# A two-layer hybrid trunk on one core: more seven-product chunks in the Down stages, a split wait at the block heads, and dilated copies ahead of a split

## What is computed

```python
def conv_ffn(h, w_up, conv_w, conv_b, w_down):
    u = h @ w_up                       # 2048 -> 11264
    ...                                # causal depthwise convolution of width 3
    gate, val = jnp.split(u, 2, axis=-1)
    return (jax.nn.silu(gate) * val) @ w_down   # 5632 -> 2048
```

## Time and profile before

| what | value |
|---|---|
| median of 3 runs | 2505.23 us (2504.09 to 2505.72) |
| the profiled execution, device time | 2504.78 us |
| its span in the profile | 2503.0 us |
| TensorE matmuls | 2495.3 us busy, 11847 |
| VectorE | 2106.8 us busy, 84% |
| ScalarE | 1422.0 us busy, 57% |
| granted TensorE clock | 1.00, the 2.4 GHz level, in every slice |

### The profile page before, as it was taken

The page is one execution under the profiler, slowest core; times in us unless marked ns, Lnnn a source line. Parts: engine busy times, 40 slices in busy tenths (PEclk is TensorE's granted clock), DMA queues, the critical chain, the costliest instruction groups (busy, mean ns, idle before and its releaser), DMA issues.

```text
span 2503.0 us, 30597 instructions
## 1 busy us (share of the span) xinstructions
PE 2495.3 (100%) x11847; PEld 2093.8 (84%) x11847; DVE 2106.8 (84%) x2373; ACT 1422.0 (57%) x1535; POOL 28.9 (1%) x36
## 2 busy tenths in 40 slices
PE   9999999999999999999999999999999999999999
PEld 8988988888888888888888888888888888888887
DVE  6656666999999999998778888776699999999998
ACT  6545555655656566556545545544566665666654
POOL 1000000000000000000000000000000000000000
PEclk9999999999999999999999999999999999999999
DMA  8554554646455557576556666654465655645654
GB/s 282 185 159 159 185 194 137 233 152 235 168 195 193 190 187 245 169 227 192 157 162 188 187 202 182 187 168 152 141 231 172 221 183 170 217 168 202 238 173 161
DMA packets 362227, 472.28 MB, mean 189 GB/s; under 512 B 18997, under 2 KB 215813, under 8 KB 361968
## 3 DMA queue, kind: packets, MB, share of 16 engines
q1 hardware_dynamic: 360448, 465.64, 56.9%
q0 software_dynamic: 1408, 4.76, 0.6%
q10 hardware_dynamic: 240, 0.10, 0.0%
HBM read 468.31 MB, written 3.68 MB: 189 GB/s over the span
## 4 chain that ended last, share of the span: by engine, by line
PE 93%; DVE 3%; ACT 2%; issue 1%; DMA 1%; SPq 0%
PE psum L1907 41%; PE psum L1911 20%; PE psum L1793 8%; PE psum L1794 8%; PE psum L1800 8%; PE psum L2005 1%; DVE w_lo L1078 1%; PE psum L1918 1%; PE psum L1920 1%; PE psum L1919 1%; PE psum L2130 1%; DMA w_raw<-in_f_w_up 1%; PE psum L2094 0%; PE psum L2128 0%; PE psum L1749 0%
## 5 line engine op out<-in xcount | busy, mean ns | idle before, releaser
L1907 PE MATMUL psum<-w_hi,xT 128*128 128x512 f32 x4016 | 1000.4, 390 | 0.3 <-DVE phase L1141 0.3
L1907 PEld LDWEIGHTS psum<-w_hi,xT 128*128 128x128 f32 x4016 | 751.5, 188 | 155.6 <-DVE phase L1141 0.7
L632 ACT ACTIVATE w_hi<-w_raw 128x2048 fp32r<-128x2048 f32 (+1 forms) x342 | 618.7, 1816 | 365.2 <-PE psum L1911 267.6
L1078 DVE TENSOR_TENSOR w_lo<-w_raw,w_hi 128x2048 fp32r<-128x2048 f32 (+1 forms) x342 | 732.1, 2162 | 57.6 <-ACT w_hi L632 57.2
L1911 PE MATMUL psum<-w_lo,xT 128*128 128x512 f32 x2008 | 523.8, 389 | 0.1
L1911 PEld LDWEIGHTS psum<-w_lo,xT 128*128 128x128 f32 x2008 | 376.8, 188 | 79.1 <-DVE w_lo L1078 1.0
L1793 PE MATMUL psum<-w_hi,xT 128*128 128x512 f32 (+1 forms) x1008 | 362.0, 369 | 0.0
L1794 PE MATMUL psum<-w_hi,xT 128*128 128x512 f32 (+1 forms) x1008 | 355.9, 363 | 0.0
L1086 DVE TENSOR_TENSOR w_lo<-w_raw,w_hi 128x2048 fp32r<-128x2048 f32 (+1 forms) x118 | 255.9, 2180 | 54.8 <-ACT w_hi L643 54.5
L643 ACT ACTIVATE w_hi<-w_raw 128x2048 fp32r<-128x2048 f32 (+1 forms) x118 | 215.3, 1830 | 104.1 <-PE psum L1911 58.8
L1070 DVE TENSOR_TENSOR w_lo<-w_raw,w_hi 128x2048 fp32r<-128x2048 f32 (+1 forms) x98 | 188.7, 1941 | 59.5 <-ACT w_hi L621 59.0
(11 more groups left out here) (199 smaller groups left out, 1887.5 us busy)
## 6 DMA issues: line engine op xcount, KB each, us to landing
w_raw<-in_f_w_up SPq DMA_DIRECT2D x352, 512.0 KB, 4.9
w_raw<-in_f_w_down SPq DMA_DIRECT2D x176, 512.0 KB, 5.1
w_raw<-in_b_w_qkv SPq DMA_DIRECT2D x192, 256.0 KB, 4.0
w_raw<-in_a_w_qkv SPq DMA_DIRECT2D x94, 512.0 KB, 4.5
w_raw<-in_b_w_qkv SPq DMA_DIRECT2D x256, 128.0 KB, 2.6
w_raw<-in_a_w_o SPq DMA_DIRECT2D x16, 1024.0 KB, 5.0
w_raw<-in_b_w_qkv SPq DMA_DIRECT2D x32, 512.0 KB, 6.3
w_raw<-in_b_w_o SPq DMA_DIRECT2D x16, 1024.0 KB, 5.0
```

The source lines that it names most:

```text
L632: nc.scalar.activation(w_hi[:, slot, cols], w_raw[:, slot, cols], ACT.Copy).then_inc(hi_ready, 1)
L1078: nc.vector.tensor_tensor(w_lo[:, slot, cols], w_raw[:, slot, cols], w_hi[:, slot, cols], ALU.subtract).then_inc(lo_ready, 1)
L1907: pe.matmul(o, x[:, h, P * m:P * (m + 1)], hi, start=start and h == 0, stop=False)
```

## The change

Three edits.

First, the form of the Down passes: groups of two where there were groups of three, so pass 0 has seven and pass 1 eight seven-product chunks. They now stand at pairs 6, 8, 10, 12, 14, 16, 18 and at 3, 6, 8, 10, 12, 14, 16, 18. The stage has 59 entries instead of 57.

Second, the first operation of `combine` increments a semaphore of its own, `p6_out`. TensorE waits for that at the head of an Up block and of Down, and for `combined` only before the second half of the head's first plain chunk (`upper_free`), eight matmuls later.

Third, in VectorE's `b_head` the copy `b_take` stands ahead of the split of entry 6.

```diff
-DOWN_ENTRIES = [(what, p, j) for p, form in enumerate(((6, (2, 2, 3, 3, 2, 3)), (3, (3, 2, 2, 3, 3, 2, 3)))) for what, j in down_pass(*form)]
+DOWN_ENTRIES = [(what, p, j) for p, form in enumerate(((6, (2, 2, 2, 2, 2, 2, 3)), (3, (3, 2, 2, 2, 2, 2, 2, 3)))) for what, j in down_pass(*form)]
...
-                chain.step(nc.vector.tensor_tensor(u[:, 1, :], p6, u[:, 0, :], ALU.add))
-                chain.settle()
+                nc.vector.tensor_tensor(u[:, 1, :], p6, u[:, 0, :], ALU.add).then_inc(p6_out, 1)
+                dve.wait_ge(p6_out, tg + 1)
...
                 for e in range(B_HEAD):
                     if e == 0 and is_turn(h, 0):
                         split_b(c + LEAD)
+                    if e == 3:
+                        b_take(c + e, h, odd)
                     if e + LEAD + 1 == B_ONES[0]:
                         b_add_weights(c + B_ONES[0], c + B_SUMS[0])
                     split_ahead(c, e)
...
-                    if e == 3:
-                        b_take(c + e, h, odd)
...
-            def plain_square(c, x, own, start, stop, high_made, low_made):
+            def plain_square(c, x, own, start, stop, high_made, low_made, upper_free=None):
                 high_made()
                 for half, i, tile in SQUARE:
+                    if half == 1 and i == 0 and upper_free is not None:
+                        upper_free()
...
+                def upper_free():
+                    at_least(pe, combined, tg)
...
             def up_block(layer, n, c, t):
                 tg, odd = UP_BLOCKS * layer + t, t % 2
-                if t > 0:
-                    pe.wait_ge(combined, tg)
+                at_least(pe, p6_out, tg)
...
                     if e == 0:
-                        pe.wait_ge(combined, last)
+                        pe.wait_ge(p6_out, last)
...
                     elif what == "std":
-                        plain_square(c + e, x, own, j == 0, False, high_made, low_made)
+                        def upper_free():
+                            pe.wait_ge(combined, last)
+
+                        plain_square(c + e, x, own, j == 0, False, high_made, low_made, upper_free if e == 0 else None)
```

More of the change, by code:

```diff
@@ L357, in trunk @@
         mix_ready, mix_hi, mix_lo = sem("mix_ready"), sem("mix_hi"), sem("mix_lo")
-        p1_out, combined, u_summed = sem("p1_out"), sem("combined"), sem("u_summed")
+        p1_out, p6_out, combined, u_summed = sem("p1_out"), sem("p6_out"), sem("combined"), sem("u_summed")
         dve_chain = sem("dve_chain")
@@ L1978, in fast_sum, with up_entry_of @@
                 low(x[1], 1, c, 3, psum[:, own + 1, :]).then_inc(used, 1)
-            def up_entry_of(c, t, e, own, other):
+            def up_entry_of(c, t, tg, e, own, other):
                 def high_made():
@@ L1988, in up_entry_of @@
                 what, j = UP_ENTRIES[t][e]
+                def upper_free():
+                    at_least(pe, combined, tg)
                 x = [xT[:, 2 * j + i, :, :] for i in range(2)]
                 if what == "std":
-                    plain_square(c, x, own, j == 0, 2 * j + 2 == KB, high_made, low_made)
+                    plain_square(c, x, own, j == 0, 2 * j + 2 == KB, high_made, low_made, upper_free if j == 0 else None)
                 else:
@@ L2023, in up_block @@
                         pe.wait_ge(val_taps, tg)
-                    up_entry_of(c + e, t, e, up_bank(layer, odd), up_bank(layer, 1 - odd))
+                    up_entry_of(c + e, t, tg, e, up_bank(layer, odd), up_bank(layer, 1 - odd))
                     if t == 0:
```

## The result

The changed kernel takes 2515.79 us in the median of 6 runs (2513.3 to 2518.24), the kernel before 2505.25 in runs beside it: ratio **1.0043**, 95% interval 1.003 to 1.0056. It is slower, by 10.5 us. A second set of runs on another occasion gave 2515.17 against 2505.59, ratio 1.0039 (1.0025 to 1.0052).

The account below looks back on a forecast made before the run. TensorE, busy over the whole span, bounds the kernel, until VectorE's lead in Down runs out. 2504.8 - 2.7 - 0.3 - 1.1 + 12.1 = 2512.8, on the median's scale 2513.2, stated as 2513.0 us; range 2508.0 to 2517.0.

Parts of the forecast that it names:

- 12 matmuls, -2.7 us: Down stages: one more seven-product chunk per pass, two passes, two layers, takes 12 matmuls of 0.2265 us off TensorE.
- VectorE's run of 11.45 us: Down, group of two: VectorE needs 11.45 us without an idle, TensorE 10.20, so each run eats 1.25 us of lead.
- The waits, 11.5 us: TensorE waits before chunks 14, 16, 18 of Down: 2.96 us in pass 0, 2.79 in pass 1, two layers.
- hand-over and restart: Extra loss in the Down passes around TensorE's waits, estimated at 0.15 us per pass, 0.6 us in all.
- Nothing is carried on: After chunk 18 VectorE idles some 4.1 us against 3.3 to 3.5 lacking, so pass 1 and the dilated heads begin as before.
- Head's wait 0.3: Head of an Up block and of Down: waiting for the first extras operation only removes the L1141 wait, gain 0.3 us.
- dilated copies 1.1: Dilated head 0: the bank copy ahead of the 2.29 us split removes TensorE's 1.07 us wait, gain 1.1 us.
- cost 0: Dilated heads 1 to 7: softmax starts 0.9 us later but has 3.9 us of cover; at most 6 us without it.
- Rival 1: Chunks 12 to 18 of each Down pass: VectorE's run fits within its lead, nothing stalls, 2501.1 us; chance 0.08.
- rival 4: VectorE's Down run costs full instruction durations, 12.0 us, losing 5.3 us a pass, about 2522 us; chance 0.02.
- Rival 2: Down "one" entries: TensorE's tight wait is the low weights, not the mixed copy; about 2504.7 us, no change; chance 0.06.
- Rival 3: Late loads stall VectorE's 24 sums after runs of two, 0.3 us each, 7 us more, 2520 us; chance 0.09.

Follow-up runs that it names:

- pass0_only: The changed kernel with the old Down form in pass 1, so the new form in pass 0 alone: 2509.41 us against 2505.59 for the kernel before, ratio 1.0015.
- copy_first: The changed kernel with VectorE's mixed copy L1470 ahead of the split of the same "one" entry: 2514.19 us against 2505.85 for the kernel before, ratio 1.0033.

## Why the prediction was right

Forecast 2513.0 (2508.0 to 2517.0), slower; measured 2515.79. Term by term:

- **12 matmuls, -2.7 us.** 11835 of them, as counted.
- **VectorE's run of 11.45 us.** It is 11.45 after, in every dense stretch, and the leads of 2.04 and 2.21 us at chunk 10 run out where they were said to, before chunk 14. Twelve waits, three per pass.
- **The waits, 11.5 us.** 11.4 by the distances of starts. The hand-over and restart was set at 0.15 per pass and came out larger. It comes with each of the twelve waits and not once a pass: after a wait the next two matmuls start 961.42 to 961.96, 0.54 us, where two spacings are 0.45, and the lag shrinks over the rest of the entry. The Down stages as a whole, by the starts of their first and last plain chunks, grew by 10.0 us net of the 2.7 saved, so 12.7 gross: 11.4 of waits and 1.3 of restarts. Forecast 12.1.
- **Nothing is carried on.** True for the passes (`pass0_only`). Not true at the end of layer 0: "and so do the dilated heads" failed. The prediction counted the lead that VectorE has to win back, and not that its freeing of a slot also starts the loads of the first dilated chunk. These were issued 3.3 us later relative to TensorE, ScalarE and VectorE waited for them, and the combine stood behind. This gave the wait L1749, 0.2 to 1.5 us.
- **Head's wait 0.3, dilated copies 1.1.** Both waits are gone; by starts they were 0.5 and 1.2. The seven later heads' "cost 0" held.

Sum by the profiles: -2.7 + 12.7 + 0.35 (L1749, by starts) - 0.5 - 1.2 = 8.6, against 8.5 measured. The medians of runs differ by 10.5 and 9.6. The profiled execution of the changed kernel was the fastest of its six. In its second profile, span 10.7 us over that of the kernel before, the Down stages and the three small terms are as in the first, but the L1749 wait is 1.0 us larger and the first 60 us are 1.3 us longer. So the forecast of 7.8 us was 0.7 below what the edits cost in the first profile. The medians lie 1 to 2 us higher still. These two things vary between the profiles by enough for that, and the one at the start of the program has nothing to do with the change; but the executions without a trace can't show that it was they.

**The rivals.** Rival 1 (the run fits) and rival 4 (full durations, by the Trainium skill's "VectorE: DVE Perf Modes", section "The TRN2 errata") are refuted by the run's 11.45 us: with 12.0 the waits would have been 5.3 us a pass, they were 2.7 to 3.0. (The run has twelve instructions, not eleven; their durations do sum to 12.0.) Rival 2 (the low weights are the tight wait) is refuted for this order by the 0.10 us between L1470 and TensorE's start, and `copy_first` shows that the low weights are right behind. Rival 3 (late loads) was wrong in its place, the sums of the dense run, and right in kind at the end of layer 0.

## What to carry to other kernels

When an edit shifts work from the bounding engine to one that is nearly full, compare the two over one period of the densest pattern, by start times, and then count how many periods in a row the measured lead can pay for. An engine that is busy 93% on average can still run out, and the same work in another order cost 6.9 us here without one instruction more. Then ask what the late engine frees late: a load that waits for its slot lands as much later, and whatever stands behind its consumer in an engine's queue is late with it.

## What the runs showed of the hardware

GpSimd and VectorE slow each other on float32 tensor-tensor operations in these stages: a 512-column add on VectorE took 0.84 us beside GpSimd and 0.69 without, a 2048-column subtraction 2.55 and 2.28. A 128-column subtraction took VectorE 0.28 us, GpSimd 0.46 where VectorE was idle, and GpSimd 2.38 when it started 0.2 us behind a 2048-column split of VectorE; it then ended 0.3 us after the split, and the split kept its 2.27 us:

```profile
1032.18 0.46 POOL L603 TENSOR_TENSOR phase<-phase 128x128 f32<-128x128 f32 x1 [5.90 <-DVE mixT L1477]
```

That is how it looks when the one that starts second waits for the first; by what path they meet no run here tells. The granted TensorE clock stayed at 1.00, its 2.4 GHz level, through waits of 1.1 us every 11.45 us.
